# Attention with unscaled probabilities: the inverse sums applied to the outputs of a pair of heads

## The reference, cut to what matters

```python
s = jnp.einsum('bqgrd,bkgd->bgrqk', qi, k, preferred_element_type=jnp.float32) * scale
p = jax.nn.softmax(s, axis=-1).astype(v.dtype)
return jnp.einsum('bgrqk,bkgv->bqgrv', p, v)
```

## Time and profile before

| | us |
|---|---|
| median of 3 runs (1083.26 to 1086.16) | 1084.48 |
| span of the profiled execution, first to last instruction | 1080.7 |
| MLA attention, first scores to first output projection | 357.2 to 396.3 |
| GQA attention, first scores to first output projection | 749.9 to 825.3 |

### The profile page before, as it was taken

The page is one execution under the profiler, slowest core; times in us unless marked ns, Lnnn a source line. Parts: engine busy times, 40 slices in busy tenths (PEclk is TensorE's granted clock), DMA queues, the critical chain, the costliest instruction groups (busy, mean ns, idle before and its releaser), DMA issues.

```text
span 1080.7 us, 14047 instructions
## 1 busy us (share of the span) xinstructions
PE 920.4 (85%) x5603; PEld 491.9 (46%) x5603; DVE 349.6 (32%) x909; ACT 295.9 (27%) x696; POOL 85.2 (8%) x96
## 2 busy tenths in 40 slices
PE   4999988777888889966999987997999965999994
PEld 1455645554644545543332326654545542333324
DVE  0422005645548640040110113474663140110112
ACT  2311023243345640041210112223673051110210
POOL 2400000101100001040000001000000141000002
PEclk9899998977889899967999997997899977999997
DMA  9999999843377202236899978014000326799925
GB/s 386 427 425 387 374 378 415 326 173 124 117 278 281 106 1 76 101 120 230 350 424 423 425 306 330 20 62 182 1 1 1 115 95 258 317 427 416 418 106 186
DMA packets 36339, 258.98 MB, mean 240 GB/s; under 512 B 3408, under 2 KB 3552, under 8 KB 21424
## 3 DMA queue, kind: packets, MB, share of 16 engines
q1 hardware_dynamic: 20448, 198.27, 45.6%
q0 software_dynamic: 12224, 47.01, 11.6%
q10 hardware_dynamic: 3600, 12.78, 2.9%
HBM read 236.73 MB, written 54.87 MB: 270 GB/s over the span
## 4 chain that ended last, share of the span: by engine, by line
PE 70%; DVE 9%; DMA 7%; ACT 7%; issue 4%; POOL 1%; PEld 1%; SPq 0%; DVEq 0%; POOLq 0%; ACTq 0%; PEldq 0%
PE ps L494 21%; PE ps L655 13%; PE ps L677 8%; PE ps L902 6%; DMA U<-expert_rows 3%; PE ps L508 3%; PE ps L639 3%; PE ps L457 2%; PE ps L731 2%; DMA ring<-w_in 2%; PE ps L533 2%; PE ps L515 2%; ACT hT L1046 1%; DMA expert_rows<-U 1%; ACT U L1026 1%
## 5 line engine op out<-in xcount | busy, mean ns | idle before, releaser
L655 PE MATMUL ps<-ring,U 128*32 128x512 f32 x1200 | 166.3, 592 | 0.0
L494 PE MATMUL ps<-U,ring 128*128 128x384 f32 x320 | 106.4, 489 | 2.7 <-DVE U L1465 1.4
L655 PEld LDWEIGHTS ps<-ring,U 128*32 128x32 f32 x1200 | 47.5, 110 | 85.3 <-issue 85.3
L677 PE MATMUL ps<-ring,U 128*32 128x512 f32 x672 | 85.7, 594 | 0.0
L494 PEld LDWEIGHTS ps<-U,ring 128*128 128x128 f32 x320 | 59.6, 189 | 46.9 <-issue 5.0
L655 PE MATMUL ps<-U 128*32 128x512 f32 x168 | 73.1, 592 | 0.0
L655 PE MATMUL ps<-hT,U 128*32 128x512 f32 x168 | 73.1, 592 | 0.0
L457 PE MATMUL ps<-ring,cond_w 128*32 128x384 f32 x512 | 59.6, 592 | 15.8 <-ACT cond_w L958 8.7
L902 PE MATMUL ps<-ring,hT 128*128 128x384 f32 x192 | 63.2, 488 | 1.7 <-issue 0.9
L639 PE MATMUL ps<-small,U 128*128 128x128 f32 x192 | 31.8, 319 | 38.4 <-DMA U<-expert_rows 36.1
L494 PE MATMUL ps<-hT,ring 128*128 128x384 f32 x192 | 63.3, 488 | 0.9 <-issue 0.8
(11 more groups left out here) (295 smaller groups left out, 1309.6 us busy)
## 6 DMA issues: line engine op xcount, KB each, us to landing
ring<-w_in SPq DMA_DIRECT2D x102, 1536.0 KB, 11.0
expert_rows<-w_in POOLq DMA_DIRECT2D x16, 2048.0 KB, 86.3
U<-expert_rows SPq DMA_DIRECT2D x24, 512.0 KB, 6.4
expert_rows<-U ACTq DMA_DIRECT2D x24, 512.0 KB, 9.1
hT<-w_in SPq DMA_DIRECT2D x6, 1536.0 KB, 12.1
U<-w_in SPq DMA_DIRECT2D x6, 1536.0 KB, 15.5
small<-small_in SPq DMA_DIRECT2D x1, 3147.5 KB, 37.2
xT<-x_in SPq DMA_DIRECT2D x1, 1536.0 KB, 16.8
```

The lines of the kernel that those rows point to most:

```text
L494: ins = mm(out, lhs(k), rhs(k), start=(k == 0), stop=(k == n - 1))
L655: ins = mm(ps[q:q + 32, r, :], xgT[:, r, P * k + q:P * k + q + 32], w[e][:, c:c + 512], start=(k == 0), stop=(k == DC - 1))
L677: ins = mm(ps[q:q + 32, 6 + h, :], actT_of[i % NR][:, P * j + q:P * j + q + 32], w[e][:, c:c + 512], start=(j == 0), stop=(j == 1))
```

## The change

The rows that are turned are now the plain exponentials: DVE's inverse and scaling of each unit go away. DVE inverts the six sums of a pair in one instruction. PE spreads the inverse sums of a pair over partitions into PSUM bank 7: for each tile and head a matmul with the sum's column, repeated 64 times, as the stationary operand and the identity as the moving one. DVE copies that bank to the output buffer and multiplies it by the values' result. The copies of turned units are shared: head a's on ACT, head b's on DVE. The waits of ACT on its own instructions go: the banks are freed by `e_ready`, `pt_act` and `pt_dve` themselves. `Pb` has six places (two new ones lie over memory that is no longer used). At the start of the program two semaphores, `cond_ready` and `fold_ready`, become one, `cond_and_fold`.

```diff
+        mP = [m_att[0][:, 384 * i:384 * i + 384] for i in range(4)] + [region(HM * 512 + 4 * HM * VM + 384 * i, 384)[0] for i in range(2)]
+        gP6 = [gP[:, 384 * i:384 * i + 384] for i in range(4)] + [region(NT * 1536 + HKV * 512 + 3072 + 384 * i, 384)[0] for i in range(2)]
+        N_P = 6
...
-                    job((kind, "s", u), "A")
-                    job((kind, "s", u + 1), "A")
+                    job((kind, "s", u), "A", "e_ready")
+                    job((kind, "s", u + 1), "A", "e_ready")
                 if u >= AHEAD:
-                    job((kind, "pT", u - AHEAD), "A")
-                    job((kind, "pT", u - AHEAD + 1), "A")
+                    job((kind, "pT", u - AHEAD), "A", "pt_act")
+                    job((kind, "pT", u - AHEAD + 1), "D", "pt_dve")
...
+        def turned_piece(PTb, b, v):
+            h, t = unit(v)
+            pt = PTb[:, 896 * (h % 2):896 * (h % 2) + 896]
+            if not t:
+                return pt[:, 0:P], b[:, 0:P]
+            return pt[:, P:].rearrange("p (k q) -> p k q", k=3)[:, :, P * (t - 1):P * t], b[:, 0:384].rearrange("p (k q) -> p k q", k=3)
...
 # PE
-                            pe.wait_ge(S["p_ready"], base + v + 1)
+                            pe.wait_ge(S["e_ready"], base + v + 1)
...
-                pe.wait_ge(S["pt_ready"], base + 2 * NT * (k + 1))
                 pair = pairs + k
-                if k >= 2:
-                    pe.wait_ge(S["o_ready"], pair - 1)
                 rows = [slice(0, 64), slice(64, 128)]
+                pe.wait_ge(S["inv_ready"], pair + 1)
+                if pair:
+                    pe.wait_ge(S["o_ready"], pair)
+                for t in range(NT):
+                    for i in range(2):
+                        u = 6 * k + 2 * t + i
+                        mm(ps[rows[i], 7, TILE[t]], rs[:, u:u + 1].broadcast_to([P, 64]), ident, start=True, stop=True)
+                pe.wait_ge(S["pt_act"], NT * (pair + 1))
+                pe.wait_ge(S["pt_dve"], NT * (pair + 1))
...
 # ACT
-                    if u >= 4:
-                        after((kind, "pT", u - 4))
+                    if u >= N_P:
+                        after((kind, "pT", u - N_P))
...
-                    act.wait_ge(S["e_ready"], base + u + 1)
-                    act.sem_inc(S["free_act"], 1)
...
-                    act.copy(out, src).then_inc(S["pt_ready"], 1)
-                    act.wait_ge(S["pt_ready"], base + v + 1)
-                    act.sem_inc(S["free_act"], 1)
+                    act.copy(*turned_piece(PTb, b, v)).then_inc(S["pt_act"], 1)
...
                     if u >= AHEAD:
                         turned(u - AHEAD)
-                        turned(u - AHEAD + 1)
...
 # DVE
-                        link(dve.reciprocal(rs[:, v:v + 1], rs[:, v:v + 1]))
-                        p = Pb[:, 384 * (v % 4):384 * (v % 4) + nk]
-                        ts(p, p, rs[:, v:v + 1], None, MUL).then_inc(S["p_ready"], 1)
...
+                def turned(v):
+                    h, t = unit(v)
+                    b = take(kind, "pT", v)
+                    if t == 0 and h >= 2:
+                        dve.wait_ge(S["pv_done"], base // NT + h // 2 * 2)
+                    dve.tensor_copy(*turned_piece(PTb, b, v)).then_inc(S["pt_dve"], 1)
+
+                def inverse(k):
+                    dve.wait_ge(S["e_ready"], base + 6 * k + 6)
+                    dve.reciprocal(rs[:, 6 * k:6 * k + 6], rs[:, 6 * k:6 * k + 6]).then_inc(S["inv_ready"], 1)
+
+                def pair_out(k):
+                    dve.wait_ge(S["pv_done"], base // NT + 2 * k + 2)
+                    link(dve.tensor_copy(out[:, k, :], ps[:, 7, 0:T]))
+                    tt(out[:, k, :], ps[:, 5 + (pairs + k) % 2, 0:T], out[:, k, :], MUL).then_inc(S["o_ready"], 1)
+
+                for u in range(0, n_u + AHEAD, 2):
                     if u < n_u:
+                        largest(u)
+                        largest(u + 1)
+                    if u >= AHEAD:
+                        turned(u - AHEAD + 1)
+                    if u and u % 6 == 0 and u <= n_u:
+                        inverse(u // 6 - 1)
+                    if u >= 12 and u % 6 == 0:
+                        pair_out(u // 6 - 2)
+                for k in range((n_u + AHEAD - 2) // 6 - 1, heads // 2):
+                    pair_out(k)
```

More of the change, by code:

```diff
@@ L229, in build, with job @@
         jobs = []
-        def job(name, by):
-            jobs.append((name, by))
+        SIGNAL = {"A": "free_act", "D": "free_dve"}
+        def job(name, by, signal=None):
+            jobs.append((name, by, signal or SIGNAL[by]))
         STEPS = [(2, False), (1, True), (2, True), (0, True)]
@@ L495, in project, with attention @@
                 return ins
-            def attention(kind, heads, q_of, k_of, v_of, places):
-                Pb, PTb = places[:2]
+            def attention(kind, heads, q_of, k_of, v_of, places, Pb):
+                PTb, _, rs = places[1:]
                 base = 0 if kind == "mla" else NT * HM
@@ L518, in attention, with values @@
                     if done > 0 and done % 6 == 0:
-                        values(done // 6 - 1, base, pairs, v_of, PTb)
-                values(heads // 2 - 1, base, pairs, v_of, PTb)
-            def values(k, base, pairs, v_of, PTb):
-                pe.wait_ge(S["pt_ready"], base + 2 * NT * (k + 1))
+                        values(done // 6 - 1, pairs, v_of, PTb, rs)
+                values(heads // 2 - 1, pairs, v_of, PTb, rs)
+            def values(k, pairs, v_of, PTb, rs):
                 pair = pairs + k
-                if k >= 2:
-                    pe.wait_ge(S["o_ready"], pair - 1)
                 rows = [slice(0, 64), slice(64, 128)]
+                pe.wait_ge(S["inv_ready"], pair + 1)
[7 more added lines that the diff above has]
+                pe.wait_ge(S["pt_dve"], NT * (pair + 1))
                 pt = [PTb[:, 896 * i:896 * i + 896] for i in range(2)]
@@ L623, in moe @@
                 turn_tokens(l, 1)
-                for by in "AD":
-                    pe.wait_ge(free_of[by], max([n for o, n in emptied[:at[0]] if o == by]))
+                for signal in ("free_act", "free_dve"):
+                    pe.wait_ge(S[signal], max([n for o, n in emptied[:at[0]] if o == signal]))
                 pe.wait_ge(S["mod_ready"], len(PARTS))
@@ L928, in _ @@
             n_chain, n_taken = [0], [0]
-            mine = [j for j, (_, by) in enumerate(jobs) if by == "A"]
+            mine = [j for j, (_, by, _) in enumerate(jobs) if by == "A"]
             def link(ins):
@@ L957, in _ @@
             act.wait_ge(S["cond_cleared"], 1)
-            A(cond3[:, :, 0:2], sm("cond").rearrange("p (k n) -> p k n", k=DC), ACT.Silu).then_inc(S["cond_ready"], 1)
+            A(cond3[:, :, 0:2], sm("cond").rearrange("p (k n) -> p k n", k=DC), ACT.Silu).then_inc(S["cond_and_fold"], 1)
             def squares(l, i):
@@ L997, in shift_of_tile, with attention @@
                     A(hT[:, c, TILE[t]], hT[:, c, TILE[t]], ACT.Identity, bias=b).then_inc(S["h_tile"], 1)
-            def attention(kind, heads, places):
-                Pb, PTb, nm, rs = places
+            def attention(kind, heads, places, Pb):
+                _, PTb, nm, rs = places
                 base = 0 if kind == "mla" else NT * HM
@@ L1317, in _ @@
             n_chain, n_taken = [0], [0]
-            mine = [j for j, (_, by) in enumerate(jobs) if by == "D"]
+            mine = [j for j, (_, by, _) in enumerate(jobs) if by == "D"]
             def link(ins):
@@ L1444, in attention @@
                 n_u = NT * heads
-                for u in range(n_u + 1):
-                    if u < n_u:
[L1447 to L1452, removed]
-                        link(dve.reciprocal(rs[:, v:v + 1], rs[:, v:v + 1]))
-                        p = Pb[:, 384 * (v % 4):384 * (v % 4) + nk]
-                        ts(p, p, rs[:, v:v + 1], None, MUL).then_inc(S["p_ready"], 1)
-                    w = v - 10
-                    if w >= 0 and w % 6 == 0:
-                        pair_out(w // 6, pairs, base, out)
@@ L1460, in attention, with largest @@
[L1460 to L1465, removed]
+                def largest(u):
+                    after(kind, "s", u)
+                    dve.tensor_reduce(nm[:, u:u + 1], bank(index[(kind, "s", u)])[:, 0:KEYS[unit(u)[1]][1]], AX.X, MAX, negate=True).then_inc(S["max_ready"], 1)
```

41 lines of the change are left out of this document (17 added, 24 removed).

## The result

The changed kernel takes 1075.37 us (median of 13 runs, 1068.81 to 1076.26) against 1082.13 for the kernel before on the same chip: ratio 0.9929, 95% interval 0.991 to 0.9948. A second series on another occasion gave 0.9945 (0.9917 to 0.9973). The time fell by 6 to 8 us. The profile of e6_nowait_six is of a slow execution (1157 us, granted clock 0.797) and isn't used.

The account below looks back on a forecast made before the run. ACT was taken to bound each pair at 8.17 us. Pairs -1.4, heads -3.3, tails +1.3 and clock falls -2.7 gave -6.1 us on the 1080.7 span, so 1074.6, with 3.8 to the median 1078.4; range 1073.5 to 1084.8.

Parts of the forecast that it names:

- ACT sets the 8.17 us, through its waits on itself: Pairs before the change: ACT never waits for work; some 0.2 us of waiting on itself behind each of twelve instructions.
- ACT at 4.4 us, DVE at 4.7 after: Work per pair after the change: 4.4 us on ACT and 4.7 us on DVE, neither being the bound.
- What is late next: Pairs: DVE's output step delays tile 1's maxima, then exponentials, ACT's copy, second transpose; 8.17 to 8.0 us, -1.4 in all.
- Spread 0.75 us in steps of two: PE, each pair: twelve added matmul instructions run side by side as six steps of 0.11 to 0.13 us.
- Rival 4: The spread's instructions don't run side by side and cost PE double: 8.75 us per pair, 1090.1 us; chance 0.09.
- Tails +0.63 each: From last but one values to output projection: 8.1 us instead of 7.50 in each attention, together +1.3 us.
- Heads -3.3 us: Up to the first values, without inverse and scaling: -1.6 in MLA, -1.7 in GQA; bounds -2.0 and -4.4.
- Falls of the clock, -2.7 us: GQA: two of three falls go, through shorter PE idle time and spread matmuls before the values; bounds 0 and -4.1.
- Rival 1: The clock falls as before, as 0.7 us of idle time before the values stays: 1081.1 us; chance 0.18.
- Rival 2: DVE's output step is hidden; pairs run at PE's 6.3 us (GQA) and 7.3 (MLA): 1065.4 us; chance 0.09.
- Rival 3: Nothing gained: ACT's exponentials stay 0.88 us apart, periods become 8.5 us: 1083.7 us; chance 0.14.
- At nothing: Parts put at no effect: merged start semaphore, deeper Pb, renamed waits; starts behind the attentions all shift along.

Follow-up runs that it names:

- e6_nowait_six: The kernel before without ACT's waits on itself and with six places of Pb instead of four; ratio to before 0.9847.
- e1_nowait: The kernel before with only ACT's waits on itself dropped; pair 6.82 us, ratio to before 0.9865.
- e5_later: The changed kernel with DVE's output step moved behind the maxima of tile 1; pair 7.24 us, ratio to before 0.9889.
- e7_selfwait: The changed kernel with ACT's waits on itself put back, without the raising of free_act behind them; pair 8.23 us, ratio to before 0.9953.
- e4_nospread: The changed kernel with the spread matmuls left out for all but each attention's first pair; pair 7.21 us, ratio to before 0.9834.
- e9_six: The kernel before with only six places of Pb instead of four; pair 8.17 us, ratio to before 0.9976.

## Why the prediction was right

The time (1078.4 forecast, 1075.4 measured; -6.1 us forecast, -6.8 between the medians, -7.7 by the ratio) and its sign came out. The mechanism of the pairs is right. That the total fits so well is in part luck: within the attentions the terms came to -12.8 us in the first profiles and -7.4 in the second ones, and the rest of the program, put at nothing, added 0.1 and 5.6 us to the spans. Step by step:

- *ACT sets the 8.17 us, through its waits on itself.* Right, shown by e1_nowait: 6.82 with nothing else changed. The size was short: 0.31 and 0.23 us each instead of 0.2.
- *ACT at 4.4 us, DVE at 4.7 after.* Measured 4.29 and 4.84 busy.
- *What is late next.* Right in mechanism and nearly in size: maxima at 2.93 us from zero (3.04 forecast), exponentials at 3.56 and 4.13 (3.66 and 4.30), period 7.86 and 7.94 (8.0). e5_later proves the place. The link behind them is right too: in all 16 periods of the two profiles the second transpose starts 0.14 to 0.15 us behind the end of ACT's copy, and in e7_selfwait it moves with that copy. PE's second scores of tile 2, behind the first exponential, are close beside it: in GQA the copy holds the second transpose back by 0.07 us only (0.18 behind the first, 0.11 where nothing holds it), in MLA by 0.16 (0.27 behind the first), and that is the 0.08 by which MLA's periods are longer. The 0.14 us of the forecast come from the maxima, 0.11 early, and small differences behind them.
- *Spread 0.75 us in steps of two.* Right (0.7), and wholly on the path (e4_nospread). Rival 4 is out.
- *Tails +0.63 each.* Measured +0.5.
- *Heads -3.3 us.* Under-sized: -7.3 in the first profiles, -4.5 between the second ones (14.53 + 14.51 against 11.44 + 13.06), both beyond its bound of -4.4. The term depends on when the clock rises, which differs from one execution to the next; in GQA's second profiles, at 0.61 and 0.55, the head gave 1.5.
- *Falls of the clock, -2.7 us.* Right in direction; three to none and one to none is -4.1 and -1.55. Of my two reasons the spreads as ordinary matmuls aren't needed: without them (e4_nospread) no fall came either. The shorter stops of PE remain, not shown by themselves. Rival 1 is out in these profiles.
- *Rival 2* (output step hidden) is what e5_later makes: 7.24, not PE's 6.3; what sets the 7.24 was not looked into. *Rival 3* is out: exponentials are 0.57 us apart.
- *At nothing.* The deeper `Pb` isn't quite nothing (e9_six, 0.9976), and the end of GQA to the end of the program grew by 1.1 to 1.7 us, where I had everything shift along; the cause is open.

The prediction priced the parts within the whole, and never asked what each would be worth alone. The scaling's place costs: the spread left out takes 0.65 us off a pair, DVE's output step moved takes 0.62 off (the two weren't put together), and what it saves is work of an engine that wasn't the bound. The whole gain of a pair is the waits', and the rest of the change gives back about a half of the time that they are worth (0.9865 to 0.9929 or 0.9945). Not all of the gain in time lies in the pairs: e7_selfwait is at 0.9953 with pairs of 8.23.

In the Trainium skill ("TensorE: Matmul & The Clock Gate", Part 4) transposes don't count as activity. The prediction set against it that the new tails would then fall to the lower clock. In the tails of the changed kernel PE has transposes and a wait alone for 2.7 us (382.74 to 385.48; the prediction has 3.6), and the granted clock stayed at 1.00 in both profiles. That doesn't bear the rule out, and since falls did come behind PE's stops in the kernel before, it doesn't settle it either.

## What to carry to other kernels

An in-order engine that waits for its own last instruction, only to raise a counter, pays for it each time; let the instruction raise the semaphore that the other side waits for. When a change bundles such a repair with a rearrangement of the work, run the repair alone first: here it was worth double the bundle. After a bound moves, look at what program order puts ahead of the first instruction of the next round; moving one call by two units was worth 0.62 us a pair.

## What the runs showed of the hardware

- A wait of ACT on its own exponential costs 0.13 us; with a separate instruction that raises a semaphore behind it, 0.31; at a copy of 384 columns both cost 0.23.
- From the end of ACT's copy to the start of the transpose that waits for it: 0.14 to 0.15 us, in all 16 periods of the changed kernel's two profiles.
- Twelve matmul instructions of 128 columns with one repeated column as stationary operand, in alternating halves of the array's columns, take 0.68 to 0.71 us at the full clock, some 0.12 for two: the repetition costs nothing beside the values' own 0.13 for two.
- Executions of one kernel differ by up to 13 us (1075.2 to 1088.0 for the kernel before) while its pairs at the full clock keep to 0.1 us; changes of a few us are seen in a period first and in the median later.
